# Two transformer blocks on one core: the order of the low and high parts, of the router stretch, and the experts' gate and up as one 512-column operand

## What is computed

```python
# block one, per layer
h = rms_norm(x, g); proj = h @ w_in                 # latents, GQA q/k/v, pool, gate logits
o_mla = mla_branch(...); o_gqa = gqa_branch(...); o_pool = pool_branch(...)
x = x + (g0*(o_mla@w_bm) + g1*(o_gqa@w_bg) + g2*(o_pool@w_bp)) @ w_out
u = depthwise_conv(rms_norm(x, g2) @ w_up); x = x + (silu(u_gate) * u_val) @ w_down
# block two, per layer
mix = (sigmoid(ga)*(ya@w_bd) + sigmoid(gb)*(yb@w_bs)) @ w_o     # two attentions
x = layer_norm(ALPHA*x + mix)
group, two experts = route(x)                       # 4 groups of 8 experts, 2 experts in one group
ffn = sum over experts: (silu(x@w_g) * (x@w_u) * weight) @ w_d  # 1024 -> 256 -> 1024
ple = sigmoid(x @ w_ple_gate) * (p @ w_ple)
x = layer_norm(ALPHA*x + ffn + ple)
```

## Time and profile before

| | |
|---|---|
| profiled execution | 2161.98 us |
| its span | 2159.7 us |
| median of three runs | 2169.36 us |
| TensorE / VectorE / ScalarE / GpSimd busy | 91% / 72% / 53% / 1% |
| mean granted TensorE clock | 0.952 |
| loaded | 420 MB, mean 196 GB/s |

### The profile page before, as it was taken

How to read it: one execution, slowest core, us unless ns; L and a number is a source line. 1 busy time by engine, 2 the same in 40 slices (tenths; PEclk the granted TensorE clock), 3 DMA queues, 4 the chain that set the end, 5 groups by cost and what they waited for, 6 DMA issues and landing times. The chain is left out here.

```text
span 2159.7 us, 29943 instructions
## 1 busy us (share of the span) xinstructions
PE 1957.0 (91%) x11440; PEld 1688.9 (78%) x11440; DVE 1556.5 (72%) x1747; ACT 1141.7 (53%) x1250; POOL 30.2 (1%) x24
## 2 busy tenths in 40 slices
PE   6988899979998999699998899999599888999996
PEld 6766799977776899677777788898477677888885
DVE  5856677878566687557757688887558676788886
ACT  3556355534554455335644576775345643677663
POOL 0000000000000000000000200000000002000000
PEclk9999999999999999899998899999799988999998
DMA  6532455545424555254353498896444353788884
GB/s 225 169 117 98 146 195 175 175 151 176 136 91 140 176 175 189 95 193 146 118 181 139 176 343 334 316 355 267 148 156 138 102 192 122 279 332 343 335 326 156
DMA packets 172066, 422.46 MB, mean 196 GB/s; under 512 B 15824, under 2 KB 68408, under 8 KB 155320
## 3 DMA queue, kind: packets, MB, share of 16 engines
q1 hardware_dynamic: 171960, 421.00, 55.0%
HBM read 419.93 MB, written 1.05 MB: 195 GB/s over the span
## 5 line engine op out<-in xcount | busy, mean ns | idle before, releaser
L228 DVE TENSOR_TENSOR w_lo<-raw,w_hi 128x2048 fp32r<-128x2048 f32 (+2 forms) x350 | 783.1, 2246 | 205.2 <-ACT w_hi L223 201.7
L223 ACT ACTIVATE w_hi<-raw 128x2048 fp32r<-128x2048 f32 (+2 forms) x350 | 655.6, 1879 | 199.9 <-PE lot L271 168.3
L269 PE MATMUL lot<-w_hi,two_xw_hi 128*128 128x256 f32 x1024 | 300.6, 294 | 19.0 <-DVE w_lo L228 11.1
L271 PE MATMUL lot<-w_hi,two_xw_lo 128*128 128x256 f32 x1024 | 289.1, 282 | 0.0
L270 PE MATMUL lot<-w_lo,two_xw_hi 128*128 128x256 f32 x1024 | 287.6, 281 | 0.0
L269 PE MATMUL lot<-w_hi,two_hT_hi 128*128 128x512 f32 (+1 forms) x544 | 222.7, 409 | 12.5 <-DVE w_lo L228 11.1
L269 PEld LDWEIGHTS lot<-w_hi,two_xw_hi 128*128 128x128 f32 x1024 | 194.4, 190 | 31.5 <-DVE w_lo L228 15.6
L270 PE MATMUL lot<-w_lo,two_hT_hi 128*128 128x512 f32 (+1 forms) x544 | 217.2, 399 | 0.0
L271 PE MATMUL lot<-w_hi,two_hT_lo 128*128 128x512 f32 (+1 forms) x544 | 217.0, 399 | 0.0
L269 PE MATMUL lot<-one_hT_hi,w_hi 128*128 128x256 f32 x704 | 201.7, 286 | 8.5 <-issue 4.8
L271 PE MATMUL lot<-one_hT_hi,w_lo 128*128 128x256 f32 x704 | 201.2, 286 | 0.0
(11 more groups left out here) (422 smaller groups left out, 3343.3 us busy)
## 6 DMA issues: line engine op xcount, KB each, us to landing
raw<-w_in SPq DMA_DIRECT2D x78, 1024.0 KB, 5.0
raw<-w_exp_gate SPq DMA_DIRECT2D x50, 1024.0 KB, 5.4
raw<-w_exp_up SPq DMA_DIRECT2D x48, 1024.0 KB, 6.4
raw<-w_exp_down SPq DMA_DIRECT2D x46, 1024.0 KB, 5.2
raw<-ffn_w_up SPq DMA_DIRECT2D x44, 1024.0 KB, 5.1
raw<-ffn_w_down SPq DMA_DIRECT2D x22, 1024.0 KB, 5.0
two_fourth<-w_exp_down SPq DMA_DIRECT2D x18, 1024.0 KB, 6.2
raw<-w_out SPq DMA_DIRECT2D x16, 1024.0 KB, 5.2
```

Of the source, the lines that this page charges most:

```text
L223: act.activation(K.hi[:, r, 0:n], self.raw(name)[:, 0:n], ACT.Copy).then_inc(K.sig["hi_ready"], 1)
L228: dve.tensor_tensor(K.lo[:, r, 0:n], self.raw(name)[:, 0:n], K.hi[:, r, 0:n].bitcast(F32), ALU.subtract).then_inc(K.sig["lo_ready"], 1)
L269: pe.matmul(out, a[0], b[0], start=start, stop=False)
L271: return pe.matmul(out, a[1], b[0], start=False, stop=stop)
```

## The change

Three kinds of edit. Block one: parts of chunks are made at other places of ScalarE's and VectorE's lists, `gq1` is multiplied after `cT` is turned, `wo10`'s tile 1 later, and the feed-forward's first step splits `U1` ahead of the taps. Block two: the router stretch in another order, `wple` ahead of `route` among the chunks, additions moved from GpSimd to VectorE, expert 0 computed from `xg` directly. Experts: a `G` chunk now holds the first four row groups of both gate and up, a `U` chunk the last four; each is loaded by two transfers, and one matmul has 512 moving columns, 256 of each matrix, into one bank.

```diff
@@ class Windows
-            sp.dma_start(ST.raw(name).rearrange("p (k c) -> p k c", k=T if name[0] == "D" else KD),
-                         self.source(name[0], group * E_G + int(name[1]))).then_inc(ST.arrived(name), 16)
+            rows = slice(0, KD // 2) if name[0] == "G" else slice(KD // 2, KD)
+            raw = ST.raw(name).rearrange("p (m k c) -> p m k c", m=2, k=KD // 2)
+            for m, w in enumerate("GU"):
+                sp.dma_start(raw[:, m, :, :], self.source(w, expert)[:, rows, :]).then_inc(ST.arrived(name), 16)
...
-        w = [v[:, 0:CHUNK].rearrange("p (k c) -> p k c", k=KD) for v in ST.parts(pe, name, i)]
-        for k in range(KD):
-            last = mm3(pe, K.ps[e % 2][:, bank, 0:D_E], [v[:, k, :] for v in (M.xw_hi, M.xw_lo)],
-                       [v[:, k, :] for v in w], k == 0, k == KD - 1)
+        w = [v[:, 0:CHUNK].rearrange("p (m k c) -> p k m c", m=2, k=KD // 2) for v in ST.parts(pe, name, i)]
+        out = K.ps[e % 2][:, 0, :].rearrange("p (m c) -> p m c", m=2)
+        for k in range(KD // 2):
+            last = mm3(pe, out, [v[:, bank * KD // 2 + k, :] for v in (M.xw_hi, M.xw_lo)],
+                       [v[:, k, :, :] for v in w], bank == k == 0, bank == 1 and k == KD // 2 - 1)
@@ block one, TensorE
-            project(K, L, ST, pe, "gq", ("gq0", "gq1"), 512, hT)
+            last = token_product(K, ST, pe, lambda t: K.ps[gq][:, t, :], hT, "gq0", True, False, 0, 4, 512)
...
+            token_product(K, ST, pe, lambda t: K.ps[gq][:, t, :], hT, "gq1", False, True, 4, 4, 512)\
+                .then_inc(L.filled("gq"), 1)
             L.wait_drained(pe, "cT")
...
-            ST.done(out_part(1, 0, 1), "wo10")
             L.wait_drained(pe, "mT1")
             out_part(0, 1, 0)
             out_part(1, 1, 0).then_inc(L.filled("wot0"), 1)
+            ST.done(out_part(1, 0, 1), "wo10")
             ST.done(out_part(0, 1, 1), "wo01")
+            transpose_tile(K, L, pe, M.tmp, "fTt0", 0, sig["n2_normed"])
             out_part(1, 1, 1).then_inc(L.filled("wot1"), 1)
@@ block one, ScalarE
+            ST.hi_to(act, "uq")
+            act_hi(K, L, act, "cT", flat(M.cT_hi[:, :, :]), lambda lot: flat(K.ps[lot][:, :, :])[:, 0:3 * S])
             ST.hi_to(act, "ukv")
...
             take("mqT0", flat(M.mqT[0:MLA_QK, 0:4, :]), rows=MLA_QK)
+            ST.hi_to(act, "g1b")
             gate_logits(0, 1)
             ga.exps(act, 2)
...
-            for u, after in enumerate(("bg0", "bg1", "bm0", None)):
+            ST.hi_to(act, "bg0")
+            for u, after in enumerate(("bg1", "bm0", "bm1", None)):
...
-                if u < 3:
-                    ma.act_out(act, u)
+                ma.act_out(act, u)
...
             act.activation(M.gates[:, :, 0:D], M.gates[:, :, 0:D], ACT.Sigmoid).then_inc(sig["late_gates"], 1)
-            ST.hi_to(act, "bm1")
-            ma.act_out(act, 3)
@@ block one, VectorE
-            ST.lo_to(dve, "window")
+            ST.lo_to(dve, "g5a")
             link(rotate(dve, link, qk, HD // 2, K.rope[:, :, 32:64], K.rope[:, :, 64:96], M.scratch, 10))
-            ST.lo_to(dve, "g5a")
...
+            ST.lo_to(dve, "g3a")
             take("gkT", flat(M.gkT[:, :, :]), lambda ps: ps[:, 0, :])
-            ST.lo_to(dve, "g3a")
+            ST.lo_to(dve, "g3b")
...
             ga.maxima(dve, link, 3)
+            ST.lo_to(dve, "g1b")
             ga.normalise(dve, link, 2)
@@ the feed-forward's walk, ScalarE (VectorE alike)
+        if i is None and e == 0:
+            ST.split_hi(act, "U1")
+            first(e, i)
+        else:
@@ block two, TensorE
+            ST.done(out_part(1, 0, 1), "wo10")
             ST.done(out_part(0, 1, 1), "wo01")
+            transpose_tile(K, L, pe, K.x, "nTt0", 0, sig["n1_normed"])
             out_part(1, 1, 1).then_inc(L.filled("wot1"), 1)
+            both("pT")
+            for c in range(2):        # pl0, pl1
...
+            route_tile(0)
+            transpose_tile(K, L, pe, K.x, "nTt1", 1, sig["n1_normed"])
+            L.claim(pe, "pg0")
+            gate_part(0, 0, 0)
+            route_tile(1)
+            gate_part(0, 1, 0)
+            ST.done(gate_part(0, 0, 1), "pg00")
             pe.wait_ge(sig["group_hot"], 1)
...             # rank
+            gate_part(0, 1, 1).then_inc(L.filled("pg0"), 1)
             project(K, L, ST, pe, "pg1", ("pg10", "pg11"), 512, hT)
...             # xg0 to xg3
+            lot = L.claim(pe, "H0a")
+            for bank, name in enumerate(("G0a", "U0a")):
...
+                    at = bank * KD // 2 + k
+                    both(f"xg{at // 2}")
+                    last = mm3(pe, out, [v[:, at, 0:P] for v in (M.xg_hi, M.xg_lo)], [v[:, k, :, :] for v in w],
+                               at == 0, at == KD - 1)
...             # slotT, weight
-            both("xg0", "xg1", "xg2", "xg3")
-            W.hidden_all(pe, "a", 0, None)
@@ block two, VectorE
+            link(add_half(1, 0, lot))
+            stats_of(K, dve, 1, 0)
+            ST.lo_to(dve, "route")
+            L.wait_filled(dve, "wot1")
+            add_half(1, 1, lot).then_inc(L.drained("wot1"), 1)
...
+            gated(0)
+            gated(1)
+            dve.tensor_copy(M.xw_lo[:, :, :], M.xg_lo[:, :, 0:P]).then_inc(sig["xw_lo"], 1)
+            ST.lo_to(dve, "G1a")
+            for c in range(2):
+                x = K.x[:, :, c * 512:(c + 1) * 512]
+                last = dve.scalar_tensor_tensor(x, x, ALPHA, M.pgate[:, c, :, :], ALU.mult, ALU.add)
@@ block two, GpSimd
-            pool.tensor_scalar(K.x[:, :, :], K.x[:, :, :], ALPHA, None, ALU.mult).then_inc(sig["pool_chain"], 1)
-                pool.tensor_tensor(x, x, M.pgate[:, c, :, :], ALU.add).then_inc(sig["pool_chain"], 1)
```

More of the change, by code:

```diff
@@ L736, in step @@
     def step(e, i):
-        first(e, i)
-        ST.split_lo(dve, f"U{e + 1}", i)
+        if i is None and e == 0:
+            ST.split_lo(dve, "U1")
+            first(e, i)
+        else:
+            first(e, i)
+            ST.split_lo(dve, f"U{e + 1}", i)
         second(e, i)
@@ L1617, in add_out, with add_halves @@
                 link(stats_of(K, dve, t, 1))
+            def add_halves(t):
+                lot = L.use[f"wot{t}"][0]
+                for c in range(2):
+                    if c == 0:
+                        ST.wait_used(dve, "wo01")
+                    else:
+                        L.wait_filled(dve, f"wot{t}")
+                    x = K.x[:, t, c * 512:(c + 1) * 512]
+                    ins = dve.tensor_tensor(x, x, K.ps[lot][:, c, :], ALU.add)
+                    if c == 0:
+                        link(ins)
+                    else:
+                        ins.then_inc(L.drained(f"wot{t}"), 1)
+                        L.wait_drained(dve, f"wot{t}")
+                    last = stats_of(K, dve, t, c)
+                    if c == 0:
+                        low_tile(0)
+                link(last)
             def low_tile(t):
@@ L1690 @@
               "g0a", "g0b", "g1a", "g1b", "g2a", "g2b", "g3a", "g3b", "bd0", "bd1", "bs0", "bs1",
-              "wo00", "wo10", "wo01", "wo11", "route", "pg00", "pg01", "pg10", "pg11", "wple"]
+              "wo00", "wo10", "wo01", "wo11", "wple", "route", "pg00", "pg01", "pg10", "pg11"]
 N_ROUTE = N_G + N_E
@@ L2095, in block_two @@
     order += [("yT", 0), ("bs0", 1), ("bs1", 0), ("bd1", 2), ("mT0", 3), ("wot0", 2), ("wot1", 1), ("mT1", 0),
-              ("pT", 3), ("nTt0", 0), ("nTt1", 3), ("rt", 1), ("pg0", 0), ("rank", 2), ("pg1", 1), ("pl0", 3), ("pl1", 2)]
-    order += [("xg0", 0), ("xg1", 1), ("xg2", 2), ("xg3", 3), ("slotT", 3), ("weight", 0), ("H0a", 0)]
+              ("pT", 3), ("nTt0", 0), ("pl0", 3), ("pl1", 2), ("nTt1", 0), ("rt", 1), ("pg0", 3), ("rank", 0), ("pg1", 2)]
+    order += [("xg0", 0), ("xg1", 1), ("xg2", 3), ("xg3", 2), ("H0a", 0), ("slotT", 3), ("weight", 2)]
     order += window_lots("a") + window_lots("z") + [("S0f", 3), ("S1f", 2), ("more", 1), ("turned", 3), ("H0b", 0)]
@@ L2101, in block_two @@
     ST = Stream(K, L, names, TWO_WIDTHS, TWO_ENDS | window_ends("a") | window_ends("z") | window_ends("b"),
-                {"route": 2}, WINDOW_TURN, {"G1a": ["G0a"], "U1a": ["H0a"], "D0a": ["H0a", "xg2"]}, "G0a", M.fourth,
+                {"route": 2} | {n: 2 for n in names if n and n[0] in "GU" and n[1].isdigit()}, WINDOW_TURN, {"G1a": ["G0a"], "U1a": ["H0a"], "D0a": ["H0a", "weight"]}, "G0a", M.fourth,
                 by_pool=())
@@ L2551, in _, with permuted @@
             act_hi(K, L, act, "pT", flat(M.pT_hi[:, :, :]), lambda lot: K.ps[lot][:, 0, :])
[L2552 removed]
             act.activation(st[:, 232:233], K.ident[:, 0:1], ACT.Sqrt)
             root_act_of(K, act, "n1", 0)
+            ST.hi_to(act, "wple")
+            act_hi(K, L, act, "nTt0", M.hT_hi[:, :, 0:P], lambda lot: by_feature(K, lot))
             ST.hi_to(act, "pg00")
[L2556 removed]
             root_act_of(K, act, "n1", 1)
[L2558 to L2564 removed]
+            def permuted(t):
+                act.wait_ge(sig["n1_normed"], 2 * T)
```

(9 more changed lines are left out.)

157 lines of the change are left out of this document (77 added, 80 removed).

## The result

2088.24 us, the median of four runs (2086.58 to 2089.68), against 2170.57 before: ratio 0.963, 95% interval 0.960 to 0.965. The prediction was 2095, range 2069 to 2127. Of the profiled execution it had said 2088; that took 2088.53, its span 2086.6. So the forecast holds, but its closeness is luck. Three errors nearly cancel: the experts' loop lost 8 to 10 us where 2 were to be gained, the 8 us taken off for waits behind the first ones were not spent there, and the router stretch gained 3 us more than forecast.

The account below looks back on a forecast made before the run. Order of work was taken to bound the kernel outside the experts' loop, TensorE inside it, DMA close behind. Gains 40.8 + 39.4 + 2 = 82, less 8, from 2162.0 gave 2088; plus 7.4, 2095 us, range 2069 to 2127.

Parts of the forecast that it names:

- the experts' loop: Block two's loop over experts: 2 us of gain in all from halving the matmul count, the split loads costing nothing.
- the 8 us taken off: Whole kernel: 8 us deducted from the summed gain for waits behind the first one at each place.
- the router stretch: Block two, from `wot1` to expert 0's first `down`: net 20.4 us gained a pass, 40.8 for both.
- (1) to (3): Block one: `gq1` over the splitting of `cT`, `g5a` ahead of the rotation, `g3a` ahead of the `gkT` copy; `g3` ends 9.3 us earlier.
- (4): Block one: `g1b` split ahead of `exps(2)` and `normalise(2)`, 5.2 us gained a pass.
- (5): Block one's merge: `bg1` moved ahead and `act_out(3)` ahead of the sigmoid, 6.6 us gained a pass.
- (6): Block one's w_out: a new wait on `wo01` with half clock, partly offset by `fTt0`, 2.4 us lost a pass.
- (7): First feed-forward step: the 1.84 us gap goes, but `down(0)` waits for later taps and silu; 1.0 us gained a pass.
- The rival of waits that re-form: Hoisted low parts push VectorE's other work, half of block one's gain, rank late again: 2129 us, chance 0.15.
- The new wait: Block two, ahead of `wo01`: TensorE stands 2.3 us, with 1.7 us of half clock behind it.
- Spare is 1.1: Experts' loop: a chunk's buffer returns every 11.4 us, landing and splitting take 10.3, so the second transfer costs nothing.
- The 7.4 us added for the median: Whole kernel: 7.4 us added to the 2088 forecast for the profiled execution, giving a median of 2095.

Follow-up runs that it names:

- block_one_alone: The kernel before with only the block-one edits and the feed-forward's first-step edit, block two untouched: 2125.2 us, ratio 0.979 to the kernel before.
- new_experts_alone: The kernel before with only the experts' new loads, chunk layout and 512-column operand: 2178.4 us, ratio 1.003 to the kernel before.
- wo01_ahead: The changed kernel with the experts as before, and both parts of `wo01` made before the merge's second turned half in both blocks: 2072.0 us.
- halves_by_partition: The changed kernel with the experts as before, but each gate or up chunk loaded by two transfers of 64 partitions: 2308.7 us.

## Why the prediction was right, and where not

**Block one**, by its own steps, in the second pass from the pass's first transposes (461.29 before, 442.58 after):

| step | predicted | measured |
|---|---|---|
| (1) to (3), up to the end of `g3` | 9.3 | 10.2 |
| (4) `g1b` | 5.2 | 5.4 |
| (5) merge | 6.6 | 6.5 |
| (6) w_out | -2.4 | -2.7 |
| (7) first feed-forward step | 1.0 | 0.7 |
| mean of both passes | 19.7 | 39.15 / 2 = 19.6 |

The measured ones are differences of the same matmul's start: the first of head pair 0's scores is at 571.37 and 542.51, which is 110.08 and 99.93 from the two starts. The waits did not re-form: from `g3` to w_out no gap is over 1 us. The window behind 644.00 loses 0.13 x 12.8 = 1.7 us of clock, the term taken. The rival of waits that re-form is out: block_one_alone keeps its whole gain. One reading in the prediction was loose: of the eight waits of the earlier trace rows four end on `w_lo`, not most, and two on other low parts.

**The router stretch.** Predicted 20.4 a pass, measured 22.3 and 22.0. The steps can be laid on the trace (add 55.17, the difference of the passes' starts): gather at 1802.7 forecast, 1801.6 measured; expert 0 done at 1815.7, and 1814.6; first `down` 1826.6, and 1826.8. Two misses cancel in the last. The new wait was 2.11, as said (2.3), but the clock stayed at 2.4 GHz behind it (1.00 in the window) where 1.7 were taken; and behind the 1.97 wait for expert 0's product, forecast as 2.1, it fell to 0.65 for 4.5 us, 1.6 lost, where nothing was taken. The prediction took half clock for given behind a gap of 2 us and more. The traces do not bear that out. The same instructions behind the same wait can go either way:

| wait, us | where | clock behind it |
|---|---|---|
| 1.84 / 1.85 | first feed-forward step, before / new_experts_alone | 1.00 / 0.72 |
| 1.97 | expert 0's product, changed, first / second pass | 1.00 / 0.65 |
| 2.05 / 2.06 | last `down` of the first pass, before / changed | 1.00 / 0.72 |
| 2.11 | `wo01` in block two, changed, both passes | 1.00 |
| 2.20 / 2.25 | expert 0's product, wo01_ahead, first / second pass | 0.63 / 0.64 |
| 2.57 | `wo01` in block one, changed, first / second pass | 0.86 / 0.87 |

The clock is the mean of the 4 to 13 us behind the wait. What decides it stays open.

The copy `xw_lo` without GpSimd beside it and the moved work of GpSimd, VectorE's timeline:

```profile
1758.73 0.69 DVE L2974 CAST two_xw_lo<-two_xg_lo 128x1024 fp32r<-128x1024 f32 x1
...
1761.55 2.35 DVE L2979 SCALAR_TENSOR_TENSOR x<-x,two_pgate 128x1024 f32<-128x1024 f32 x2
```

0.69 where it took 2.81, at the low end of the 0.7 to 1.2 taken; and 2.35 for the two multiply-adds, taken as 2.4. The Trainium skill (SBUF — State Buffer, SBUF: two separate sides) has some of VectorE's instructions share one pair of ports with GpSimd, which the one that starts first holds for its whole instruction. Both times agree with it; no run here moved the work back.

**The experts' loop** is the step that failed: "Spare is 1.1; I cost it at nothing" and "I take 2 us of gain". From the first `down` to the pass's end it took 6.3 and 4.0 us more, of which 4.0 and 4.0 lie between the first `down` and the last. The other 2.3 of the first pass stand behind the last `down`, mostly at half clock after the 2.06 of the table. The reckoning of a round of four chunks was right for 24 intervals in 30 (225.8 against 226.0), and was applied to all; the three turns took 4.4 more. The trace of before showed that turns differ: two experts take 18.8 there, not 17.1, and two loads go out together after 6 us of none; that window was not read. The Trainium skill (DMA: Bandwidth & Descriptors, Rules for kernel authors) asks for 1 MiB or more a transfer for the most bandwidth; here the 0.5 MB ones took 0.89 of the DMA engines' time for the rate that whole chunks had at 0.86, a loss, but one that between turns stays hidden. The same page's fixed cost of a DMA (Anatomy of one DMA), fitted there on transfers that GpSimd issues while SP issues these, would have made 2138 if the second half had paid it in series; 2088 refuses that.

The operand: no price per matmul that the medians show, as the 512-column row had said. Twelve take 2.76 us after as before (230 ns each). The 131 ns of the Trainium skill (TensorE: Matmul & The Clock Gate, Back-to-back issue gap) are seen in no form of 512 columns here.

**The 8 us taken off** stood for waits behind the first ones. Those did not come; the loop's 10.3 stood in their place. Terms by the profiles: 39.2 + 44.2 - 10.3 = 73.1, forecast 39.4 + 40.8 + 2 - 8 = 74.2. The total was right by a margin that had been put to another cause, and that is luck.

**The 7.4 us added for the median** are what is left of the miss, 2095 against 2088.2. They were the distance of one short execution of the kernel before from the median. The changed kernel's profiled execution is 0.3 above its own median, and its four executions lie within 3.1 us, where those of the kernel before lie within 10.

Left open: why a late chunk is whole 1.6 us later when four transfers are under way and not two, and whether it is count or row length that costs, which halves_by_partition could not part.

## What to carry to other kernels

Where TensorE stands on the low part of a chunk that landed long ago, moving that part ahead by hand gives the gap back, and the half clock behind it, as long as no other engine is the next limit: in block one it did, at `wo01` in block two it gave nothing. The new orders, with the work taken from GpSimd and expert 0 made from `xg`, were worth some 91 us here, and the matmul's shape nothing that the medians show. Reckon a transfer's spare at the turn of a loop too, not only in its middle: there loads bunch, and a chunk in two transfers is late although the mean shows room. A sum that comes out right can still have a term of the wrong sign, so run the parts alone; here that gave a kernel 16 us faster than the change.

## What had not been expected of the hardware

- Two transfers over 64 partitions each, in place of one over 128, filled the DMA engines at 240 GB/s and made the kernel 11% slower (2308.7 against 2079.0).
- Four transfers of 256 KB a chunk in place of two of 512 KB cost 6 us in 2088, although the loads had 227,256 packets for 190,392.
- The same block one, unchanged, took 7.3 us longer in another execution, mostly in four stretches of matmuls at half rate; one of them has a mean clock of 0.78 instead of 1.00 over 48 matmuls.
- A wait of 1.84 to 2.06 us was followed by the full clock in one execution or pass and by half clock in another, in front of the same instructions.
